# The last long product of a two-block transformer step, FFN down, done as seven half-size fp32 products

## What is computed

```
act  = silu(h @ w_ffn_gate) * (h @ w_ffn_up)          # 256 x 2816
x    = ALPHA * x + gate * (act @ w_ffn_down)          # the product is 256 x 2816 by 2816 x 1024
out  = layer_norm(x) * ln2_g + ln2_b
```

## Time and profile before

| | us |
|---|---|
| median of three runs | 1635.34 |
| lowest and highest run | 1632.17, 1636.71 |
| profiled execution | 1635.62 |
| its span | 1633.9 |
| mean granted TensorE clock | 0.979 of 2.4 GHz |
| PE, DVE, ACT, POOL busy in the span | 1525.3, 681.8, 381.7, 217.3 |

### The profile page before, as it was taken

One profiled execution on the slowest core, in us unless ns is written; L12 is line 12 of the kernel. 1 busy time (PEld: TensorE's weight loads), 2 busy tenths in 40 slices (PEclk: granted clock), 3 DMA queues, 4 the chain that ended last, 5 costly groups with the idle time before them and its releaser, 6 DMA issues.

```text
span 1633.9 us, 22997 instructions
## 1 busy us (share of the span) xinstructions
PE 1525.3 (93%) x9388; PEld 1042.4 (64%) x9388; DVE 681.8 (42%) x1450; ACT 381.7 (23%) x847; POOL 217.3 (13%) x364
## 2 busy tenths in 40 slices
PE   8999999999898797888998889999899999999997
PEld 4548655554676464456766578865578864888843
DVE  3206311432644343624444357777978752100003
ACT  1001154321421112332332132133443320100000
POOL 2000000000000000124223010001365520400000
PEclk9999999999999899899999899999999999999999
DMA  9444432664699999999999934432153422544431
GB/s 320 158 155 154 154 103 103 220 203 188 232 407 406 406 406 412 365 417 416 416 413 416 407 112 155 141 117 103 52 219 104 155 104 103 196 149 145 152 134 49
DMA packets 124205, 370.43 MB, mean 227 GB/s; under 512 B 10555, under 2 KB 26565, under 8 KB 107589
## 3 DMA queue, kind: packets, MB, share of 16 engines
q1 hardware_dynamic: 118352, 362.04, 58.5%
q0 software_dynamic: 1280, 6.29, 1.1%
q10 hardware_dynamic: 4469, 0.62, 0.2%
HBM read 367.89 MB, written 1.05 MB: 226 GB/s over the span
## 4 chain that ended last, share of the span: by engine, by line
PE 45%; DMA 6%; DVE 4%; ACT 1%; issue 1%; SPq 0%; DVEq 0%; ACTq 0%
PE psum L2139 28%; PE psum L666 7%; DMA ring<-in_w_down 3%; DMA ring<-in_w_up 3%; PE psum L1934 2%; PE psum L1956 1%; PE psum L2133 1%; PE psum L1975 1%; PE psum L692 1%; PE psum L1918 1%; PE psum L846 1%; PE psum L2295 1%; DVE ring L1378 0%; PE psum L825 0%; PE psum L863 0%
## 5 line engine op out<-in xcount | busy, mean ns | idle before, releaser
L2139 PE MATMUL psum<-ring,area 128*128 128x512 f32 (+1 forms) x1040 | 449.2, 590 | 5.3 <-DVE area L1401 2.0
L2139 PE MATMUL psum<-area,ring 128*128 128x256 f32 (+1 forms) x1856 | 395.8, 372 | 3.8 <-DMA ring<-in_w_in 2.1
L2139 PEld LDWEIGHTS psum<-area,ring 128*128 128x128 f32 x1856 | 339.4, 190 | 49.9 <-DMA ring<-in_w_in 2.8
L2139 PEld LDWEIGHTS psum<-ring,area 128*128 128x128 f32 x1040 | 196.9, 191 | 241.4 <-issue 239.0
L666 PEld LDWEIGHTS psum<-area 128*128 128x128 f32 x1216 | 140.9, 192 | 21.4 <-issue 15.9
L666 PE MATMUL psum<-area 128*128 128x128 f32 x1216 | 149.4, 279 | 4.3 <-ACT area L1083 4.1
L2420 ACT ACTIVATE area<-psum 128x512 f32<-128x512 f32 x108 | 61.4, 598 | 392.7 <-PE psum L2139 321.9
L1934 PE MATMUL psum<-ring,area 128*32 128x256 f32 x1760 | 112.2, 400 | 23.7 <-DMA ring<-in_w_up 23.7
L1934 PEld LDWEIGHTS psum<-ring,area 128*32 128x32 f32 x1760 | 57.3, 114 | 66.4 <-issue 38.1
L2133 PE MATMUL psum<-const,area 128*128 128x128 f32 (+2 forms) x507 | 79.8, 283 | 16.7 <-DVE area L2574 5.5
L1287 DVE SCALAR_TENSOR_TENSOR area<-area,cols 128x268 f32<-128x268 f32 (+1 forms) x186 | 91.6, 492 | 6.6
(11 more groups left out here) (339 smaller groups left out, 1471.5 us busy)
## 6 DMA issues: line engine op xcount, KB each, us to landing
ring<-in_w_in SPq DMA_DIRECT2D x28, 2048.0 KB, 8.3
ring<-in_w_gate SPq DMA_DIRECT2D x55, 1024.0 KB, 15.0
ring<-in_w_up SPq DMA_DIRECT2D x55, 1024.0 KB, 15.3
ring<-in_w_down SPq DMA_DIRECT2D x53, 1024.0 KB, 15.5
ring<-in_w_ada SPq DMA_DIRECT2D x12, 2048.0 KB, 8.1
ring<-in_w_out SPq DMA_DIRECT2D x6, 2048.0 KB, 8.5
area<-in_w_down SPq DMA_DIRECT2D x11, 1024.0 KB, 17.0
ring<-in_w_ffn_gate SPq DMA_DIRECT2D x5, 2048.0 KB, 7.9
```

The costliest lines, as they stand in the source:

```text
L2139: last = nc.tensor.matmul(dst, lhs(k), rhs(k), start=first and k == 0, stop=final and k == count - 1)
```

## The change

The product of `act` (256 x 2816) and `w_ffn_down` (2816 x 1024) is divided into quarters: the tokens into two halves of 128, the output columns into two halves of 512, and the row tiles of each unit into an early and a late half. With a11, a12, a21, a22 for the quarters of act (token half, then early or late) and b11, b12, b21, b22 for those of a unit (early or late, then column half), Strassen's scheme (in the form with four sums on each side) makes seven products instead of eight:

- sums of act, by DVE as the up tiles come (`sum_act`): s1 = a21 + a22, s2 = s1 - a11, s3 = a11 - a21, s4 = a12 - s2
- sums of the weights, by DVE as the units land (`sum_down`): t3 = b22 - b12, t1 = b12 - b11 (written over b12 in the ring), t2 = t3 + b11, t4 = b21 - t2
- seven products, each in a PSUM bank of its own: P1 = a11 b11, P2 = a12 b21, P3 = s4 b22, P4 = a22 t4, P5 = s1 t1, P6 = s2 t2, P7 = s3 t3
- combined once, at the end, by DVE: first_sum = P1 (copied out by ACT), second_sum = first_sum + P6, third_sum = second_sum + P7, fourth_sum = second_sum + P5. Token tile 0 is first_sum + P2 and fourth_sum + P3, token tile 1 is third_sum + P4 and third_sum + P5.

The seven products are accumulated over the six units. t2, t3 and t4 have three sets of buffers, used in turn; one set lies in the two ring slots that the weights of this part don't use. The banks close in the order 1, 6, 7, 5, 4, 2, 3, token tile 1 is normed before tile 0, and the stores follow that order. The diff without the new semaphores, and without the new first parameter of `residual`, which now takes the name of a tile:

```diff
+        fd_tiles = [4, 4, 4, 4, 4, 2]
+        act_sums = [at(place, FFN_TILES // 2, P) for place in (0, 4096, 5504, 13824)]
+        down_sums = [kept_flat[:, 0:3072].rearrange("p (s k n) -> p s k n", s=3, k=2), at(20096, 3, 2, WIDE), at(32128, 3, 2, WIDE)]
+        first_sum, second_sum, third_sum, fourth_sum = at(28288, WIDE), at(28800, WIDE), at(29312, WIDE), at(1408, WIDE)
...
+        def quarters(n):
+            home, offset = slot_place(unit_slot[f"fd{n}"])
+            w = home[:, offset:offset + fd_tiles[n] * D].rearrange("p (k n) -> p k n", n=D)
+            k = fd_tiles[n] // 2
+            return w[:, 0:k, 0:WIDE], w[:, 0:k, WIDE:D], w[:, k:2 * k, 0:WIDE], w[:, k:2 * k, WIDE:D]
+        def act_quarters(n):
+            k0, k = sum(fd_tiles[:n]), fd_tiles[n] // 2
+            early, late = ffn_act[:, k0:k0 + k, :], ffn_act[:, k0 + k:k0 + 2 * k, :]
+            return early[:, :, 0:P], late[:, :, 0:P], early[:, :, P:SEQ], late[:, :, P:SEQ]
+        def sums_of_act(n):
+            k0, k = sum(fd_tiles[:n]) // 2, fd_tiles[n] // 2
+            return [part[:, k0:k0 + k, :] for part in act_sums]
...
-            for j in range(FFN_TILES // 2):
-                wait_drained(pe, ("fu", j))
-            long_product("fd", [f"fd{i}" for i in range(6)], ffn_act)
+            pe.wait_ge(s["mod_drained"], 12 - MOD_FIRST)
+            sevenths = {i: open_tile(("P", i), (bank,), closes_next=False)
+                        for i, bank in ((1, 4), (2, 5), (3, 6), (5, 7), (7, 0), (6, 1), (4, 2))}
+            def seventh(i, n):
+                a11, a12, a21, a22 = act_quarters(n)
+                b11, t1, b21, b22 = quarters(n)
+                s1, s2, s3, s4 = sums_of_act(n)
+                t3, t2, t4 = (down_sums[n % 3][:, j, :, :] for j in range(3))
+                lhs, rhs = {1: (a11, b11), 2: (a12, b21), 3: (s4, b22), 4: (a22, t4), 5: (s1, t1), 6: (s2, t2), 7: (s3, t3)}[i]
+                return product(sevenths[i], lambda k: lhs[:, k, :], lambda k: rhs[:, k, :], fd_tiles[n] // 2,
+                               first=n == 0, final=n == 5)
+            def closed(i, last):
+                order.close(("P", i))
+                last.then_inc(filled, 1)
+            for n in range(3):
+                pe.wait_ge(s["act_sums_ready"], n + 1)
+                unit(f"fd{n}")
+                for i in (1, 2, 3):
+                    seventh(i, n)
+                pe.wait_ge(s["down_sums_ready"], n + 1)
+                for i in (5, 7, 6, 4):
+                    last = seventh(i, n)
+                pieces_passed[0] += 1
+                last.then_inc(passed, 1)
+                unit_freed[f"fd{n}"] = passed, pieces_passed[0]
+            pe.wait_ge(s["act_sums_ready"], 4)
+            unit("fd3")
+            seventh(1, 3)
+            pe.wait_ge(s["down_sums_ready"], 4)
+            for i in (6, 7, 5):
+                seventh(i, 3)
+            pe.wait_ge(s["act_sums_ready"], 6)
+            unit("fd4")
+            seventh(1, 4)
+            unit("fd5")
+            closed(1, seventh(1, 5))
+            pe.wait_ge(s["down_sums_ready"], 5)
+            seventh(6, 4)
+            pe.wait_ge(s["down_sums_ready"], 6)
+            closed(6, seventh(6, 5))
+            for i in (7, 5):
+                seventh(i, 4)
+                closed(i, seventh(i, 5))
+            for i in (4, 2, 3):
+                seventh(i, 3)
+                seventh(i, 4)
+                closed(i, seventh(i, 5))
...
+            copy_out(("P", 1), first_sum)
+            for t in (1, 0):
...
+            def sum_act(n):
+                a11, a12, a21, a22 = act_quarters(n)
+                s1, s2, s3, s4 = sums_of_act(n)
+                link(v.tensor_tensor(s1, a21, a22, ALU.add))
+                link(v.tensor_tensor(s2, s1, a11, ALU.subtract))
+                step(v.tensor_tensor(s3, a11, a21, ALU.subtract))
+                v.tensor_tensor(s4, a12, s2, ALU.subtract).then_inc(s["act_sums_ready"], 1)
+            def sum_down(n):
+                b11, b12, b21, b22 = quarters(n)
+                t3, t2, t4 = (down_sums[n % 3][:, j, 0:fd_tiles[n] // 2, :] for j in range(3))
+                name = f"fd{n}"
+                eng.wait_ge(landed[unit_slot[name]], landed_by[name])
+                if n >= 3:
+                    which, count = unit_freed[f"fd{n - 3}"]
+                    eng.wait_ge(which, count)
+                link(v.tensor_tensor(t3, b22, b12, ALU.subtract))
+                step(v.tensor_tensor(b12, b12, b11, ALU.subtract))
+                link(v.tensor_tensor(t2, t3, b11, ALU.add))
+                v.tensor_tensor(t4, b21, t2, ALU.subtract).then_inc(s["down_sums_ready"], 1)
+            def gated_in(src, t, half):
+                part, tmp = slice(half * WIDE, (half + 1) * WIDE), ffn_tmp[:, half, :]
+                link(v.tensor_tensor(tmp, src, mod_rows[:, 3, part], ALU.mult))
+                link(v.tensor_tensor(x[:, t, part], x[:, t, part], tmp, ALU.add))
...
+                if j % 2 or j == 10:
+                    wait_drained(eng, ("fu", j - 1 if j % 2 else j))
+                    wait_drained(eng, ("fu", j))
+                    sum_act(j // 2)
+                if j == 9:
+                    sum_down(0)
+            for n in range(1, 6):
+                sum_down(n)
             eng.wait_ge(s["x_scaled"], 1 + NT)
-            summed("fd", 3, norm_rows[:, 2, :], norm_rows[:, 3, :], x, "x_ready", 2)
+            wait_drained(eng, ("P", 1))
+            gated_in(first_sum, 0, 0)
+            v.tensor_tensor(second_sum, wait_filled(eng, ("P", 6)), first_sum, ALU.add).then_inc(drain_of(("P", 6)), 1)
+            wait_drained(eng, ("P", 6))
+            v.tensor_tensor(third_sum, wait_filled(eng, ("P", 7)), second_sum, ALU.add).then_inc(drain_of(("P", 7)), 1)
+            wait_drained(eng, ("P", 7))
+            gated_in(third_sum, 1, 0)
+            gated_in(third_sum, 1, 1)
+            link(v.tensor_tensor(fourth_sum, wait_filled(eng, ("P", 5)), second_sum, ALU.add))
+            residual(("P", 5), 1, 1, 3)
+            gated_in(fourth_sum, 0, 1)
+            residual(("P", 4), 1, 0, 3)
+            moments(1)
+            normed(1, norm_rows[:, 2, :], norm_rows[:, 3, :], x[:, 1, :], "x_ready")
+            residual(("P", 2), 0, 0, 3)
+            residual(("P", 3), 0, 1, 3)
+            moments(0)
+            normed(0, norm_rows[:, 2, :], norm_rows[:, 3, :], x[:, 0, :], "x_ready", 2)
...
-            for n, (t, part) in enumerate(((0, slice(0, D)), (1, slice(0, WIDE)), (1, slice(WIDE, D)))):
+            for n, (t, part) in enumerate(((1, slice(0, D)), (0, slice(0, WIDE)), (0, slice(WIDE, D)))):
```

More of the change, by code:

```diff
@@ L387, in two_block_kernel @@
         tile = lambda place: at(place, GDN_HEADS, P)
-        kept = ring_flat[:, KEPT * SLOT:].rearrange("p (n h c) -> p n h c", n=4, h=GDN_HEADS)
+        kept_flat = ring_flat[:, KEPT * SLOT:]
+        kept = kept_flat.rearrange("p (n h c) -> p n h c", n=4, h=GDN_HEADS)
         delta = [delta_buffers([26592] * 2, tile(26592), [tile(28640)] * 2, [tile(29664)] * 2, 30688, 31712, 20096, 32736, 21120, (), 33760),
@@ L435, in two_block_kernel @@
             "rest_gate_in", "rest_up_in", "rest_down_in", "rest_h2_turned", "rest_h2_ready", "dta_in", "xdt_ready",
-            "x_ready", "x_scaled", "c_cleared", "c_cols_ready", "part_filled", "part_ready", "parts_ready",
+            "x_ready", "x_scaled", "act_sums_ready", "down_sums_ready", "c_cleared", "c_cols_ready", "part_filled", "part_ready", "parts_ready",
             "out_done", "pads_ready", "conv_ready", "channels_ready", "abs_ready",
@@ L1221, in second_block_act @@
             nc.scalar.activation(stats[:, 60:61], ones[:, 0:1], ACT.Sqrt)
-            for t in range(NT):
+            copy_out(("P", 1), first_sum)
+            for t in (1, 0):
                 root(mean_of[:, t, 1:2])
@@ L1630, in second_block_dve, with residual @@
             normed_o(0)
-            def residual(key, t, half, gate):
+            def residual(tile, t, half, gate):
                 part, tmp = slice(half * WIDE, (half + 1) * WIDE), ffn_tmp[:, half, :]
-                v.tensor_tensor(tmp, wait_filled(eng, (key, t, half)), mod_rows[:, gate, part], ALU.mult)\
-                 .then_inc(drain_of((key, t, half)), 1)
-                wait_drained(eng, (key, t, half))
+                v.tensor_tensor(tmp, wait_filled(eng, tile), mod_rows[:, gate, part], ALU.mult)\
+                 .then_inc(drain_of(tile), 1)
+                wait_drained(eng, tile)
                 link(v.tensor_tensor(x[:, t, part], x[:, t, part], tmp, ALU.add))
@@ L1657, in summed @@
                     for half in range(2):
-                        residual(key, t, half, gate)
+                        residual((key, t, half), t, half, gate)
                     moments(t)
```

## The result

The median of six runs is 1626.56 us (1623.98 to 1628.65) against 1635.72 for six runs of the kernel before on the same chip: a ratio of 0.9941 with a 95% interval of 0.9928 to 0.9954, or 9.2 us less (7.5 to 11.8). The forecast was 1626.6, 9.1 less.

The account below looks back on a forecast made before the run. PE's instruction count was taken to bound the last stretch, DVE having room. PE's end at 1616.08 (22 fewer matmuls, join +0.22) plus 8.57 and 0.19 for the ending and 1.72 around the span gave 1626.6 us, range 1624.0 to 1630.5.

Parts of the forecast that it names:

- The product: Down product on PE: 154 matmuls in the trace instead of 176, at 0.4306 us each, saving 9.47 us.
- The rival that the time does not go with the count: Down product: more bank turns and waits cost PE 5.9 us, giving 1632.5 us; chance 0.06.
- that of the half clock: Down product from fd3 on: idle times between bank turns halve PE's clock, costing 30 us, giving 1656.7; chance 0.03.
- The join: Between last up tile and down product: two more waits add 0.22 us, PE starting at 1549.77.
- about 0.11 for each: Price in us per wait behind PE's wait for the last up tile, read from 0.14 with few and 0.69 with five.
- the rival of the clock at the join: Start of down product: PE's idle time lowers its clock, losing 1.9 us, giving 1628.5; chance 0.13.
- the four things that were to show the prediction right: 154 matmuls at 0.43 without idle; join idle near 1.7; first weight sums in time; P3's residual 0.2 to 0.4 after PE.
- The first set of weight sums: DVE's sums for fd0, before the last up tile is filled: 1.22 us per instruction, done about 1547.0, 1.1 us cover.
- fd5's sums: DVE's weight sums for the last-landing unit: done at 1593.8, wanted by PE at 1597.1, 3.3 us cover.
- The ending: After PE's end: DVE starts P3's residual 0.29 us later where 0.10 is usual, 0.19 late, then 8.57 as before.
- ACT's copy of P1: In the ending: ACT copies P1 out in about 0.55 us, well ahead, with no table load following.
- The sum: Whole kernel: span 1624.84 us, 1626.56 with the 1.72 around it, 9.1 less than the profiled execution before.

Follow-up runs that it names:

- The eighth product: Changed kernel with P2 made twice, the second time into a bank nobody reads, sums and waits kept: median 1636.62 us, ratio to before 0.9996.
- The doubled set: Changed kernel with four more DVE instructions of 128 x 1024 ahead of fd0's weight sums: median 1632.58 us, ratio to before 0.9978.
- The one instruction fewer: Changed kernel with P2 in bank 3, plus third_sum and P5 added first and gated once in DVE's ending: median 1626.20 us, ratio to before 0.9932.

## Why the prediction was right, and which step failed

*The product: right.* 22 fewer matmuls by 0.4306 were to save 9.47; 75.78 - 66.33 is 9.45. The eighth product brings it back. The rival that the time does not go with the count falls with the same two runs, and so does that of the half clock: seven banks in turn, 1.00 throughout.

*The join: failed in sign.* It was to be 1.49 + 0.22 = 1.71 and is 1.04, so the term is -0.45 in place of +0.22, inside its ends. The step that failed is "about 0.11 for each" wait behind the releasing one. The price is right where it was read, with ten waits ahead, and the change took these ten away: the new join opens with two. The prediction counted what was added behind the wait and not what was removed ahead of it. In the kernel before, seven behind cost 0.91 with ten ahead; in the kernel after they cost 0.23 with two. No run gave the kernel after its ten waits back, so that their removal is the whole of the difference is argued and not shown. So one of the four things that were to show the prediction right, an idle time near 1.7 at the join, did not come, and the same step made the rival of the clock at the join look nearer than it was. The rival has its own answer in two joins of before: with two more behind the idle time is 1.70, where 1.71 was forecast for the kernel after, with ten more it is 1.88, and PE kept 1.00, with 75.78 and 75.79 for the product.

*The first set of weight sums: right, and the narrow place.* In the kernel after, DVE's timeline has it like this (the cover is the time from the end of the set, L1758 at 1548.19, to the filling of the last up tile at 1550.57; the last two rows belong to fd5):

```profile
1544.54 1.23 DVE L1755 TENSOR_TENSOR ring<-ring 128x1024 f32<-128x1024 f32 x1 [5.20 <-DMA ring<-in_w_ffn_down]
...
1548.19 1.23 DVE L1758 TENSOR_TENSOR ring<-ring 128x1024 f32<-128x1024 f32 x1
1550.68 0.69 DVE L1772 TENSOR_TENSOR area<-psum,area 128x512 f32<-128x512 f32 x1 [1.26 <-PE psum L2267]
...
1592.75 0.69 DVE L1755 TENSOR_TENSOR area<-ring 128x512 f32<-128x512 f32 x1 [4.17 <-DMA ring<-in_w_ffn_down]
...
1594.80 0.69 DVE L1758 TENSOR_TENSOR area<-ring,area 128x512 f32<-128x512 f32 x1
```

The set is done at 1549.42 and the tile filled at 1550.57: 1.15 of cover where 1.1 was forecast, each instruction 1.22 to 1.23. The doubled set shows that behind this cover every us counts, and then costs the clock too. The Trainium skill (SBUF — State Buffer, section "SBUF: two separate sides") has a DVE instruction with two SBUF inputs and a GpSimd instruction that reads SBUF shut each other out for whole instructions; the run with POOL busy agrees (0.42 became 2.46). fd5's sums, forecast as the tightest of the others, end at 1595.49, and PE, which wants them 47.3 after its own start, at 1598.9, is not idle.

*The ending: right, a little short.* The residual of P3 was to start 0.29 after PE's end and starts 0.38 after. Against the usual 0.10 that is 0.28 late, forecast 0.19. The one instruction fewer gave it back. ACT's copy of P1 takes 0.60 at 1597.37, forecast 0.55, and no table load follows.

*The sum.* -9.45 for the product, -0.45 for the join, +0.28 for the ending: -9.62, and the stretch shows -9.61. The forecast of 9.1 was 0.5 too small there: 0.67 from the join, less 0.09 from the ending. That is less than the runs of one kernel scatter (1623.98 to 1628.65), so that the median came within 0.1 of 1626.6 is luck.

## What to carry to other kernels

Where one engine is the bound by its count of instructions and another is idle beside it, trading instructions between them paid one to one here, as long as the first traded piece was ready at the join; look for that place, since lateness there was paid twice, as waiting and as clock. A price read at a join belongs to the whole list of waits there: count what a change removes ahead of the releasing wait as well as what it adds behind. And before DVE gets work with two SBUF inputs, look whether POOL is idle in that stage.

## What the runs showed of the hardware that was not expected

- Waits long met are not free at a join: 0.11 us each for the first seven behind the releasing one with ten or more ahead, and next to nothing with none ahead. The cause is open.
- PE kept its clock at 1.00 after idle times of 1.04 to 1.88 at this join, and lost 2.5 to 2.7 us after 4.12 and 4.71. Before an earlier product 1.99 cost 1.9; there PE had been idle for 0.69 as well, 2.05 earlier, and no run separates the two.
- DVE's 128 x 256 sums beside POOL took 1.81 to 2.57 where they take 0.42 alone. The delay is near the length of one POOL instruction (2.46), also for the 128 x 1024 (3.37 where it takes 1.22). POOL's instructions had only this one size in that run.
